# Attention layer: the last gate pieces moved into late steps by column parts, and each woven step cut into three half pieces

## The chip, the cores and the metric

The kernel runs on one core of a Trainium2 chip. The metric is the device time of one execution in microseconds, the median of several runs. The core has five engines with queues of their own: TensorE (PE, its weight loads are PEld), VectorE (DVE), ScalarE (ACT), GpSimd (POOL) and SyncE (SP, which issues DMAs). They meet only at semaphores.

## What is computed

Four layers, each `x <- x + RMSNorm(mixer(RMSNorm(x)))`, for 1024 tokens of a prompt and 8 single tokens of a second group: 1032 columns, in three parts of 344. The mixers are a gated MLP, attention, a recurrence and again a gated MLP. The change touches the attention layer alone:

```python
def project_b(h, w_in):
    z = h @ w_in                    # q (1024), k (128), v (128), gate (1024)
    ...
def mixer_b_prompt(h, w_in, sinks, w_out):
    q, k = rope(q, pos), rope(k, pos)
    scores = jnp.einsum('bnqkgd,bnskd->bnkgqs', qb, kk) * (HEAD_DIM ** -0.5)   # blocks of 128, window 128
    p = sink_softmax(scores, mask[None, :, None, None], sinks.reshape(N_KV_HEADS, Q_PER_KV))
    o = jnp.einsum('bnkgqs,bnskd->bnqkgd', p.astype(vv.dtype), vv)
    out = (o * jax.nn.silu(g)) @ w_out
```

Everything is fp32. A product is made of three matmuls of split operands: high weights by high activations, high weights by low activations, low weights by high activations.

## The kernel before

**Weights.** They come in units of 128 output features x 1024 inputs (512 KB). A ring of three slots holds them: SyncE loads `w_raw`, ScalarE writes the high half (`w_high`), VectorE the low half (`w_low`). SyncE loads unit u as soon as the result of unit u - 3 is counted (`results_at_end`).

**Units of the attention layer.** Units 0 and 1 are k and v, 2 to 5 are q and gate tiles 0 and 1, 6 to 17 in turn two q tiles and two gate tiles (6, 7 are q; 8, 9 gate; 10, 11 q; 12, 13 gate; 14, 15 q; 16, 17 gate), 18 to 25 the output product. Units 6 to 17 are not run whole but as 36 *pieces*, three per unit, one for each part of 344 columns. Piece p has 24 matmuls (8 input tiles x 3) and one of two PSUM banks; it needs piece p - 2 to be read by VectorE (`read_piece`, L1695, whose work is L1702).

**The woven loop.** 32 steps, i = 0 to 31: four groups of heads (two tiles of q) by eight blocks of 128 tokens. In step i TensorE (L862) issues a piece if the step has one, then `values(i - 1)` (L808), then the step's second piece, then `scores(i + 2)` (L777), then `turns(i)` (L795), the transposes of the probabilities. `piece_range` (L371) gives steps one and two pieces in turn, 1.5 in the mean, until piece 35 in step 22. Steps 24, 26 and 31 and the end of the loop have parts of the first two units of the output product (`out_part`, L824), steps 23 to 28 the attention of the 8 single tokens (`sample_...`).

Each step goes round the engines. VectorE: `maxima(i + 1)` (L1708, adds the mask and takes maxima, signals B; the scores two steps on need it, for their PSUM banks), the read of a first piece, `outputs(i - 1)` (L1731, times the gate), `lows(i - 2)`, the read of a second piece, `sums(i + 1)` (L1724); then for a unit that ended in the step before, `w_low` of two units on and, for a q unit, `rotate_q` (three products over 1032 columns, L1654 to L1657). ScalarE: `copies(i - 1)` (L1244, transposed probabilities out of PSUM, what values wait for), `exps(i + 1)` (L1235), `highs(i - 1)` (L1251), and for a unit that ends in this step `unit_end` (L1213): for q four DMAs that swap halves of q for the rotation (L1198), for an odd gate tile both tiles' silu (L1211, its table is another than the exponentials'), and always `w_high` of two units on. GpSimd scales the exponentials by the sums (L503), which turns need. SyncE loads the single tokens' keys behind unit 18's weights, once all q are rotated.

Each engine works its list in order, so what waits holds all behind it.

## Time and profile before

| | before |
|---|---|
| median of 3 runs | 2394.38 us (2393.76 to 2395.12) |
| the profiled execution's own time | 2395.22 us |
| its span | 2393.4 us |
| TensorE busy | 2324.8 us, 97% |
| VectorE busy | 1227.2 us, 51% |
| ScalarE busy | 891.0 us, 37% |
| GpSimd busy | 91.8 us, 4% |
| woven loop of the attention layer | 883.0 to 1152.4 us |

A row of the timeline is: start us, duration us, engine, line, operation, output<-input, shape, count, and in brackets the idle time before it with what ended it. The duration of a matmul reaches beyond the start of the next; what it costs is read from start to start. PEclk is the granted clock as a share of 2.4 GHz.

### The profile page before, as it was taken

What the parts mean: (1) busy time and instruction counts of PE and PEld (TensorE: products, weight loads), DVE (VectorE), ACT (ScalarE), POOL (GpSimd) and SP (SyncE); (2) the same over time, 40 slices, a digit from 0 to 9 for tenths busy, and PEclk for the clock granted to TensorE, in tenths of its full rate; (3) what the DMA queues carried; (4) which work ended last, traced back from release to release, by engine and by line L of the source; (5) the groups of instructions that cost most, each with busy time, mean ns of one, the idle gap of its engine ahead of it and who ended that gap; (6) DMA issues with size and microseconds to landing.
All of it is one profiled execution on the core that took longest, in us unless ns stands there. A gap on an engine that the chain in (4) does not pass through costs nothing.

```text
span 2393.4 us, 35999 instructions
## 1 busy us (share of the span) xinstructions
PE 2324.8 (97%) x15487; PEld 2238.3 (94%) x15487; DVE 1227.2 (51%) x1753; ACT 891.0 (37%) x1278; POOL 91.8 (4%) x44
## 2 busy tenths in 40 slices
PE   8999999999999899997999999999999999999997
PEld 7999999999999798886888999989999999999996
DVE  4444444454433756665256887364444544545235
ACT  6223332333332535455353366353223332333221
POOL 0000000000000002222000010000000000000000
PEclk9999999999999999997999999999999999999998
DMA  4111111111121331120222111322111111111213
GB/s 137 45 45 45 45 45 42 38 45 45 39 96 45 125 113 54 45 72 10 107 83 70 45 45 45 118 74 87 45 54 36 45 45 37 44 45 45 89 46 107
DMA packets 58494, 145.86 MB, mean 61 GB/s; under 512 B 8904, under 2 KB 29528, under 8 KB 58328
## 3 DMA queue, kind: packets, MB, share of 16 engines
q1 hardware_dynamic: 53056, 135.34, 17.2%
q10 hardware_dynamic: 5280, 8.22, 1.3%
q8 instruction: 122, 2.00, 0.3%
q14 instruction: 36, 0.29, 0.0%
HBM read 121.47 MB, written 18.37 MB: 58 GB/s over the span
## 4 chain that ended last, share of the span: by engine, by line
PE 82%; DVE 9%; ACT 4%; DVEq 3%; ACTq 1%; issue 1%; DMA 1%; SPq 0%
PE ps L528 61%; PE ps L552 7%; PE ps L773 4%; PE ps L686 2%; PE ps L610 2%; DVE x L1430 1%; DVE l_acc L1427 1%; PE ps L818 1%; DVE w_lo L1388 1%; PE ps L790 1%; PE ps L829 1%; PE ps L679 1%; ACT l_h_hi L1013 1%; DVE l_hs L1925 1%; DVEq L1429 1%
## 5 line engine op out<-in xcount | busy, mean ns | idle before, releaser
L528 PE MATMUL ps<-l_h_hi,w_hi 128*128 128x344 f32 x2448 | 526.5, 323 | 2.6 <-DVE w_lo L1388 2.6
L528 PE MATMUL ps<-l_h_lo,w_hi 128*128 128x344 f32 x2448 | 519.7, 320 | 0.0
L528 PE MATMUL ps<-l_h_hi,w_lo 128*128 128x344 f32 x2448 | 516.2, 319 | 0.0
L528 PEld LDWEIGHTS ps<-l_h_hi,w_hi 128*128 128x128 f32 x2448 | 408.9, 188 | 6.8 <-DVE w_lo L1388 3.5
L528 PEld LDWEIGHTS ps<-l_h_lo,w_hi 128*128 128x128 f32 x2448 | 414.0, 189 | 0.0
L528 PEld LDWEIGHTS ps<-l_h_hi,w_lo 128*128 128x128 f32 x2448 | 407.8, 188 | 0.0
L1388 DVE TENSOR_TENSOR w_lo<-w_raw,w_hi 128x1024 fp32r<-128x1024 f32 x182 | 226.1, 1243 | 249.8 <-ACT w_hi L962 240.5
L962 ACT ACTIVATE w_hi<-w_raw 128x1024 fp32r<-128x1024 f32 x182 | 190.8, 1049 | 117.6 <-DMA w_raw<-in_wu 79.4
L1505 DVE TENSOR_TENSOR l_tmp<-ps,rx 128x1032 f32<-128x1032 f32 x64 | 78.9, 1232 | 285.5 <-PE ps L528 285.4
L528 PE MATMUL ps<-l_y_lo,w_hi 128*128 128x344 f32 x816 | 173.2, 320 | 0.0
L528 PE MATMUL ps<-l_y_hi,w_hi 128*128 128x344 f32 x726 | 154.7, 321 | 0.8 <-DVEq L1939 0.8
L528 PE MATMUL ps<-l_y_hi,w_lo 128*128 128x344 f32 x726 | 153.1, 319 | 0.0
L1107 ACT ACTIVATE l_tmp<-l_tmp 128x1032 f32<-128x1032 f32 x32 | 34.2, 1067 | 303.9 <-DVEq L1546 303.9
L528 PEld LDWEIGHTS ps<-l_y_lo,w_hi 128*128 128x128 f32 x816 | 137.9, 189 | 0.0
L528 PEld LDWEIGHTS ps<-l_y_hi,w_hi 128*128 128x128 f32 x726 | 121.6, 188 | 1.7 <-DVEq L1939 1.1
L528 PEld LDWEIGHTS ps<-l_y_hi,w_lo 128*128 128x128 f32 x726 | 120.9, 188 | 0.0
L1112 ACT ACTIVATE l_tmp<-l_tmp 128x1032 f32<-128x1032 f32 x32 | 34.2, 1068 | 226.6 <-DVEq L1551 226.6
L1091 ACT ACTIVATE l_v<-l_v 128x1032 f32<-128x1032 f32 x32 | 34.1, 1067 | 214.9 <-DVEq L1527 214.9
L503 POOL TENSOR_TENSOR l_sc<-l_sc,l_rq 128x1024 f32<-128x1024 f32 x32 | 71.3, 2227 | 1075.1 <-DVE l_rq L1729 1075.1
L1505 DVE TENSOR_TENSOR l_v<-ps,rx 128x1032 f32<-128x1032 f32 x28 | 34.5, 1233 | 120.2 <-PE ps L528 118.1
L773 PE MATMUL ps<-l_h_hi,w_hi 128*128 128x344 f32 x288 | 95.8, 333 | 0.0
L552 PE MATMUL ps<-l_y_lo,w_hi 128*128 128x344 f32 x288 | 92.6, 322 | 0.0
(245 smaller groups left out, 3597.2 us busy)
## 6 DMA issues: line engine op xcount, KB each, us to landing
w_raw<-in_wu SPq DMA_DIRECT2D x182, 512.0 KB, 3.5
x_save<-x SPq DMA_DIRECT2D x9, 1376.0 KB, 6.1
x<-x_save SPq DMA_DIRECT2D x21, 516.0 KB, 6.9
l_sw<-l_q ACTq DMA_DIRECT2D x32, 129.0 KB, 2.8
out_y<-x SPq DMA_DIRECT2D x6, 688.0 KB, 3.6
x<-in_xt SPq DMA_DIRECT2D x4, 688.0 KB, 10.6
x<-in_xt SPq DMA_DIRECT2D x5, 516.0 KB, 6.3
x<-in_xt ACTq DMA_DIRECT2D x3, 516.0 KB, 3.7
```

What stands on the lines that cost most here:

```text
L503: nc.gpsimd.tensor_tensor(L.sc[:, i % 2], L.sc[:, i % 2], L.rq[:, i % 2].rearrange("p (h o) -> p h o", o=1).to_broadcast([P, 4, 2 * WIN]), ...
L528: mm = nc.tensor.matmul(ps[:, 3 * slot + ch, 0:CW], wt[:, w, k, :], mv[:, k, ch * CW:(ch + 1) * CW], start=(k == 0 and t == 0), stop=(k == ...
L552: mm = nc.tensor.matmul(ps[:, 3 * slot + ch, 0:CW], wt[:, u % W_RING, k, :], mv[:, k, part(ch)], start=(k == 0 and t == 0), stop=(k == KT ...
L610: mm = nc.tensor.matmul(ps[:, 3 * j + c, 0:CW], wt[:, (u + j) % W_RING, k, :], mv[:, k, part(c)], start=(k == 0 and t == 0), stop=(k == KT ...
L686: mm = nc.tensor.matmul(ps[:, 6 + b // 4, (b % 4) * P:(b % 4 + 1) * P], vt[:, b, :], L.ws[:, g, :], start=True, stop=True)
L773: mm = nc.tensor.matmul(ps[:, p % 2, 0:CW], wt[:, w % W_RING, k, :], mv[:, k, part(ch)], start=(k == 0 and t == 0), stop=(k == KT - 1 and ...
L962: nc.scalar.activation(w_hi[:, u % W_RING], w_raw[:, u % W_RING], ACT.Copy).then_inc(w_hi_done, 1)
L1091: nc.scalar.activation(tile_of(L.v, m), tile_of(L.v, m), ACT.Gelu_apprx_tanh)
L1107: nc.scalar.activation(L.tmp[:, 0, :], L.tmp[:, 0, :], ACT.Gelu_apprx_tanh).then_inc(L.u_act.sem, 1)
L1112: nc.scalar.activation(L.tmp[:, 1, :], L.tmp[:, 1, :], ACT.Silu).then_inc(L.g_act.sem, 1)
L1388: V.tensor_tensor(w_lo[:, u % W_RING], w_raw[:, u % W_RING], w_hi[:, u % W_RING], ALU.subtract).then_inc(w_lo_done, 1)
L1505: V.tensor_tensor(chunks(out), psum_result(slot), chunks(rx[:]), ALU.mult)
```

## The change

The 36 pieces get another plan (`STEP_PIECES`, `step_pieces`): entries are (piece, first input tile, end), so a piece can be halves of 12 matmuls. Steps 3 to 17 have three halves each: ahead of values, ahead of scores, ahead of turns. Steps 18 to 26 have one to three halves' worth, in the first two places. Pieces 30 to 35 (gate units 16 and 17) alternate between the two units, column part by column part, and run to step 26. VectorE reads a piece in the place in which it ends; in the third place the read stands behind the sums and ahead of `w_low` and `rotate_q`.

For pieces 30 to 35 silu is made by parts: VectorE's read writes half of the gate (g/2), ScalarE takes tanh of it into `L.th`, VectorE makes (tanh + 1) x g/2. The silu of tiles 6 and 7 goes. `w_high` and `w_low` of units 18 and 19 get places of their own (steps 22 and 22, 29 and 30). The output parts of 18 matmuls of steps 24 and 26 become four of 9 in steps 27 to 30; the single tokens' stages come two steps later.

```diff
@@ -73,7 +73,7 @@
     "ssq_mm": (CH,) * 3, "root": (CH,) * 3,
-    "x_back": (16 * (KT - A_EARLY), 16 * KT, 16 * KT), "in_done": (3 * MA, 2 * KT + 2, KT), "act_done": (MA, KT, 0),
+    "x_back": (16 * (KT - A_EARLY), 16 * KT, 16 * KT), "in_done": (3 * MA, 2 * KT + 2, KT), "act_done": (MA, KT - 2, 0), "gate_th": (0, 2 * CH, 0), "gate_done": (0, 2 * CH, 0),
     "y_hi_done": (0, 0, KT), "y_lo_done": (0, 1, KT), "h_free": (KT, 0, 0), "y_high": (MA, 0, 0), "y_low": (MA, 0, 0), "acc_done": (LAST + 3 * CH, 0, 0), "ysq_done": (LAST + 3 * CH,) * 3,
@@ -242,6 +242,8 @@
                 L.pts = at(n + "pts", o, [P, 2, P]); o += 1024
+                L.th = [at(n + "th0", o, [P, CW]), at(n + "th1", rope_at + 2 * TILE + 2080, [P, CW])]
+                o += CW * 4
                 assert o <= X_AT + KT * TILE
@@ -257,6 +259,7 @@
                 L.piece_read = s("piece_read")
+                L.gate_th, L.gate_done = s("gate_th"), s("gate_done")
             if kind == "c":
@@ -340,7 +343,8 @@
                 n = L.result_of(u) if L.kind == "c" else L.r0 + u - L.u0
-                results_at_end.append(3 * n + (5 if u in (L.u0, L.u1 - 3, L.u1 - 2) else 3))
+                by_parts = u in (L.u0, L.u1 - 3, L.u1 - 2) or (L.kind == "b" and u == L.u0 + 16)
+                results_at_end.append(3 * n + (5 if by_parts else 3))
@@ -368,13 +372,34 @@
-        def piece_range(i):
-
-            return range(min(36, 1 + (3 * i + 1) // 2), min(36, 1 + (3 * i + 4) // 2))
+        LATE = 30
+        HALF = KT // 2
+        STEP_PIECES = {0: ((2, 0, KT),), 1: ((3, 0, HALF),), 2: ((3, HALF, KT), (4, 0, KT)),
+                       18: ((27, HALF, KT), (28, 0, HALF)), 19: ((28, HALF, KT), (29, 0, KT)), 20: ((30, 0, HALF),), 21: ((30, HALF, KT), (31, 0, KT)),
+                       22: ((32, 0, HALF),), 23: ((32, HALF, KT),), 24: ((33, 0, KT), (34, 0, HALF)), 25: ((34, HALF, KT),), 26: ((35, 0, KT),)}
+        def step_pieces(i):
+            if i in STEP_PIECES or i > 18:
+                return STEP_PIECES.get(i, ())
+            halves = range(10 + 3 * (i - 3), 10 + 3 * (i - 2))
+            return tuple((h // 2, h % 2 * HALF, h % 2 * HALF + HALF) for h in halves)
+        def pieces_ended(entries):
+            return [p for p, _, end in entries if end == KT]
+        def late_end(i):
+            return [p for p in pieces_ended(step_pieces(i)) if p >= LATE]
         def piece_unit(p):
-            return 6 + p // 3
+            return 6 + p // 3 if p < LATE else 16 + p % 2
+        def piece_part(p):
+            return p % 3 if p < LATE else (p - LATE) // 2
@@ -383,7 +408,7 @@
-            return [piece_unit(p) for p in piece_range(i) if p % 3 == 2]
+            return [piece_unit(p) for p in pieces_ended(step_pieces(i)) if p < LATE and p % 3 == 2]
@@ -760,19 +785,21 @@
-                def piece(p):
-                    w, ch = u + piece_unit(p), p % 3
-                    if ch == 0:
+                def piece(p, first=0, end=KT):
+                    w, ch = u + piece_unit(p), piece_part(p)
+                    if ch == 0 and first == 0:
                         pe.wait_ge(w_lo_done, w + 1)
-                    if p >= 2:
-                        pe.wait_ge(*L.piece_read.at(p - 1))
-                    else:
-                        pe.wait_ge(evac[0], 3 * ((r + 6) // 2))
-                    for k in range(KT):
+                    if first == 0:
+                        if p >= 2:
+                            pe.wait_ge(*L.piece_read.at(p - 1))
+                        else:
+                            pe.wait_ge(evac[0], 3 * ((r + 6) // 2))
+                    for k in range(first, end):
                         for t, (wt, mv) in enumerate(((w_hi, L.h_hi), (w_hi, L.h_lo), (w_lo, L.h_hi))):
                             mm = nc.tensor.matmul(ps[:, p % 2, 0:CW], wt[:, w % W_RING, k, :], mv[:, k, part(ch)],
                                                   start=(k == 0 and t == 0), stop=(k == KT - 1 and t == 2))
-                    mm.then_inc(result, 1)
+                    if end == KT:
+                        mm.then_inc(result, 1)
@@ -860,32 +887,38 @@
                 for i in range(STEPS):
-                    now = [p for p in piece_range(i) if p >= 2]
-                    for p in now[:1]:
-                        piece(p)
-                    if i == 24:
+                    now = step_pieces(i)
+                    for p, first, end in now[:1]:
+                        piece(p, first, end)
+                    if i == 27:
                         pe.wait_ge(w_lo_done, u + 19)
                         pe.wait_ge(*L.piece_read.at(36))
                         pe.wait_ge(*L.Lo.at(19))
-                        out_part(0, 0, range(0, 6))
+                        out_part(0, 0, range(0, 3))
+                    if i == 28:
+                        out_part(0, 0, range(3, 6))
+                    if i == 29:
+                        pe.wait_ge(*L.Lo.at(22))
+                        out_part(0, 1, range(0, 3))
+                    if i == 30:
+                        out_part(0, 1, range(3, 6))
                     if i:
                         values(i - 1)
-                    for p in now[1:]:
-                        piece(p)
-                    if i == 23:
+                    for p, first, end in now[1:2]:
+                        piece(p, first, end)
+                    if i == 25:
                         sample_scores()
-                    if i == 25:
+                    if i == 27:
                         sample_turns()
-                    if i == 26:
-                        pe.wait_ge(*L.Lo.at(22))
-                        out_part(0, 1, range(0, 6))
-                    if i == 27:
+                    if i == 29:
                         sample_values()
...
                         scores(i + 2)
+                    for p, first, end in now[2:]:
+                        piece(p, first, end)
                     turns(i)
@@ -1232,6 +1265,15 @@
                     w_high(L.u0 + 6 + m)
+                def gate_tanh(p):
+                    act.wait_ge(*L.piece_read.at(p + 1))
+                    if p == LATE + 1:
+                        act.wait_ge(*L.rotated.at(KT))
+                    if p >= LATE + 2:
+                        act.wait_ge(*L.gate_done.at(p - LATE - 1))
+                    nc.scalar.activation(L.th[p % 2][:], L.gate[:, 6 + p % 2, part(piece_part(p))], ACT.Tanh).then_inc(L.gate_th.sem, 1)
                 def exps(i):
@@ -1265,7 +1307,13 @@
                         unit_end(j)
-                    if i == 24:
+                    if i == 22:
+                        w_high(L.u0 + 18)
+                    for p in late_end(i):
+                        gate_tanh(p)
+                    if i == 29:
+                        w_high(L.u0 + 19)
+                    if i == 26:
                         act.wait_ge(*L.ssE.at(1))
@@ -1693,17 +1741,28 @@
                 def read_piece(p):
-                    j, ch = piece_unit(p), p % 3
+                    j, ch = piece_unit(p), piece_part(p)
                     is_q, m = piece_tile(p)
                     dve.wait_ge(result, 3 * (r + 6) + p + 1)
-                    if not is_q and m >= 6 and ch == 0:
-
-                        dve.wait_ge(*L.kout.at(16 * 6))
-                    V.tensor_tensor((L.q if is_q else L.gate)[:, m, part(ch)], ps[:, p % 2, 0:CW], rx[:, part(ch)], ALU.mult
-                                    ).then_inc(L.piece_read.sem, 1)
+                    if p >= LATE:
+                        if ch == 0:
+                            dve.wait_ge(*L.kout.at(16 * 6))
+                        V.scalar_tensor_tensor(L.gate[:, m, part(ch)], ps[:, p % 2, 0:CW], 0.5, rx[:, part(ch)], ALU.mult, ALU.mult
+                                               ).then_inc(L.piece_read.sem, 1)
+                    else:
+                        V.tensor_tensor((L.q if is_q else L.gate)[:, m, part(ch)], ps[:, p % 2, 0:CW], rx[:, part(ch)], ALU.mult
+                                        ).then_inc(L.piece_read.sem, 1)
                     if ch == 2:
                         V.drain().then_inc(L.in_done.sem, 1)
                         V.drain().then_inc(evac[j % 2], 3)
+                def gate_silu(p):
+                    dve.wait_ge(*L.gate_th.at(p - LATE + 1))
+                    g = L.gate[:, 6 + p % 2, part(piece_part(p))]
+                    V.scalar_tensor_tensor(g, L.th[p % 2][:], 1.0, g, ALU.add, ALU.mult).then_inc(L.gate_done.sem, 1)
+                    V.drain()
@@ -1731,7 +1790,7 @@
                     dve.wait_ge(*L.PV.at(i + 1))
-                    if n == 0:
+                    if n == 0 and qd < 3:
                         dve.wait_ge(*L.act_done.at(2 * qd + 2))
@@ -1813,31 +1872,39 @@
                         maxima(i + 1)
-                    now = list(piece_range(i))
-                    for p in now[:1]:
+                    now = step_pieces(i) if i else ((1, 0, KT),) + step_pieces(0)
+                    for p in pieces_ended(now[:1]):
                         read_piece(p)
...
                         lows(i - 2)
-                    for p in now[1:]:
+                    for p in pieces_ended(now[1:2]):
                         read_piece(p)
                     if i + 1 < STEPS:
                         sums(i + 1)
+                    for p in pieces_ended(now[2:]):
+                        read_piece(p)
+                    for p in late_end(i - 1) if i else ():
+                        gate_silu(p)
+                    if i == 22:
+                        w_low(L.u0 + 18)
+                    if i == 30:
+                        w_low(L.u0 + 19)
                     for j in units_ended(i - 1) if i else []:
...
                             rotate_q(m)
-                    if i == 21:
+                    if i == 23:
                         sample_keys()
-                    if i == 23:
+                    if i == 25:
                         sample_maxima()
-                    if i == 24:
+                    if i == 26:
                         sample_normals()
-                    if i == 26:
+                    if i == 28:
                         sample_probs()
-                    if i == 28:
+                    if i == 30:
                         sample_outputs()
```

## Rows read from the trace of the kernel before

**Rows 1.** Busy time by stretch: steps 0-17, 18-22, 23-31; columns in the first line.
```profile
core 0: us, PE busy (x) PEld busy (x) DVE busy (x) ACT busy (x) POOL busy (x), PEclk, DMA share, GB/s
883.00:1043.20 160.20, 158.84 (x1259) 139.28 (x1257) 101.34 (x312) 86.02 (x225) 41.55 (x19) 1.00 0.18 51
1043.20:1088.70 45.50, 44.73 (x353) 39.21 (x352) 34.87 (x94) 21.80 (x59) 12.05 (x6) 1.00 0.22 61
1088.70:1152.40 63.70, 46.97 (x369) 33.77 (x367) 32.05 (x132) 35.04 (x98) 17.66 (x9) 0.73 0.02 8
```

**Rows 2.** Timeline of TensorE over a step with two pieces.
```profile
974.06 0.43 PE L773 MATMUL ps<-l_h_hi,w_hi 128*128 128x344 f32 x1
974.33 0.32 PE L773 MATMUL ps<-l_h_lo,w_hi 128*128 128x344 f32 x1
974.49 0.32 PE L773 MATMUL ps<-l_h_hi,w_lo 128*128 128x344 f32 x1
...
978.04 1.08 PE L818 MATMUL ps<-l_pt,l_vtok 128*64 128x256 f32 x8
979.06 0.42 PE L773 MATMUL ps<-l_h_hi,w_hi 128*128 128x344 f32 x1
...
983.04 1.13 PE L790 MATMUL ps<-l_kd,l_q 64*128 64x256 f32 x8
984.00 0.66 PE L804 MATMUL ps<-ident,l_sc 64*128 64x64 f32 x16
984.59 0.42 PE L773 MATMUL ps<-l_h_hi,w_hi 128*128 128x344 f32 x1
```

**Rows 3.** Timeline of TensorE: values in steps without pieces ahead of them.
```profile
1091.85 1.97 PE L818 MATMUL ps<-l_pt,l_vtok 128*64 128x256 f32 x8 [3.14 <-ACT l_pt L1248]
...
1130.39 1.97 PE L818 MATMUL ps<-l_pt,l_vtok 128*64 128x256 f32 x8 [1.11 <-ACT l_pt L1248]
...
1136.35 1.08 PE L818 MATMUL ps<-l_pt,l_vtok 128*64 128x256 f32 x8 [1.11 <-ACT l_pt L1248]
```

**Rows 4.** Timeline of VectorE: the sums of two steps that follow each other.
```profile
1139.69 0.16 DVE L1727 TENSOR_TENSOR l_rq<-l_mx 128x4 f32<-128x4 f32 x1 [1.42 <-ACTq L1242]
...
1144.45 0.16 DVE L1727 TENSOR_TENSOR l_rq<-l_mx 128x4 f32<-128x4 f32 x1 [1.41 <-ACTq L1242]
```

**Rows 5.** Timeline of VectorE: sums, low weights, rotation, the next maxima.
```profile
973.30 0.15 DVE L1727 TENSOR_TENSOR l_rq<-l_mx 128x4 f32<-128x4 f32 x1
...
973.62 1.20 DVE L1388 TENSOR_TENSOR w_lo<-w_raw,w_hi 128x1024 fp32r<-128x1024 f32 x1
974.73 2.93 DVE L1654 TENSOR_TENSOR l_sw<-l_sw,l_sin 128x1032 f32<-128x1032 f32 x1
...
978.88 1.23 DVE L1657 TENSOR_TENSOR l_q<-l_q,l_sw 128x1032 f32<-128x1032 f32 x1
980.39 0.48 DVE L1716 CUSTOM_DVE_ANT_0 l_sc<-ps,l_mask,l_sink 128x256 f32<-128x256 f32 x1 [0.28 <-issue]
```

**Rows 6.** Timeline of ScalarE behind it, and TensorE's values that wait.
```profile
982.47 0.51 ACT L1239 ACTIVATE l_sc<-l_sc,l_mx 128x256 f32<-128x256 f32 x1 [7.27 <-DVEq L1722]
...
984.82 2.46 ACTq L1198 DMA_DIRECT2D l_sw<-l_q  x4
...
988.29 1.00 ACT L1248 ACTIVATE l_pt<-ps 128x1024 f32<-128x1024 f32 x1
...
989.35 1.08 PE L818 MATMUL ps<-l_pt,l_vtok 128*64 128x256 f32 x8 [0.71 <-ACT l_pt L1248]
```

**Rows 7.** Timeline of steps 0 to 2: first piece of step 1, a copy, exponentials.
```profile
898.52 0.42 PE L773 MATMUL ps<-l_h_hi,w_hi 128*128 128x344 f32 x1
...
901.12 1.01 ACT L1248 ACTIVATE l_pt<-ps 128x1024 f32<-128x1024 f32 x1
...
913.42 0.51 ACT L1239 ACTIVATE l_sc<-l_sc,l_mx 128x256 f32<-128x256 f32 x1 [7.22 <-DVEq L1722]
```

**Rows 8.** Timeline of ScalarE in step 22: the last silu and the load ahead.
```profile
1086.63 1.28 ACT L1211 ACT_TABLE_LOAD   x1
1087.93 2.02 ACT L1211 ACTIVATE l_gate<-l_gate 128x1032 f32<-128x1032 f32 x2
```

## What I expect, and how it is worked out

> **What bounds the kernel now.** I first read the stretches: the attention layer's woven loop runs from 883.0 to 1152.4 us, 269.4 us in 32 steps. TensorE is busy for 158.84 of 160.20 us in steps 0 to 17 and for 44.73 of 45.50 us in steps 18 to 22, but only for 46.97 of 63.70 us in steps 23 to 31, and the granted clock there is 0.73 on average, so the two levels (2.4 and 1.2 GHz) take turns [rows 1]. All the rest of the span lies outside the change, so the question is only how long the 269.4 us become.
>
> Next I read one step on TensorE. A piece of 24 products takes 3.98 us from its start to that of what follows, the first product 0.27 and the others 0.16 (0.157 over many); values take 1.02, scores 0.96 ahead of turns, turns 0.59 [rows 2]. Scores with a piece behind them take 1.06: a piece starts 0.06 ahead of the end shown for values (1.08, and 1.02 to the next start), and scores show 1.13. So the work of the loop at the full clock is: 36 pieces x 3.98 = 143.3; 32 values x 1.02 = 32.6; 32 scores, 30.9; 32 turns x 0.59 = 18.9; the four parts of the output product (48 products x 0.157 and 0.21 of edges for each part) 8.4; the three sample groups about 3.6, an estimate. Sum 237.7. Of the 31.7 us that are left, 1.4 + 0.8 are idle before step 23 and 16.7 after [rows 1]. The remaining 12.8 us is what the lower clock adds: values take 1.97 us in it and not 1.08 [rows 3].
>
> What makes the idle time? Up to step 22 hardly anything: the pieces hide it. Without pieces a step is a ring of VectorE and ScalarE: maxima, then the exponentials, then the sums, and VectorE starts the next maxima only behind the sums. That ring is 4.76 us from sums to sums [rows 4]. A step of values, scores and turns alone is 2.6 us of TensorE. With half a piece it is 4.7, about what the ring needs. This is what speaks for the change.
>
> **The change, part by part.**
>
> (1) *Splitting costs edges.* A half piece is 3.98 - 12 x 0.157 = 2.1 us, so a split adds 0.18 to 0.2 us. A step of three halves instead of one and a half pieces adds 1.5 x 0.18 and the 0.10 of scores that now have a piece behind them, 0.37 us [rows 2]; 15 steps (3 to 17) give 5.6. Pieces 3, 28, 30, 32 and 34 and the two output parts of 18 products are split too: 7 x 0.18 = 1.3. Together **+6.9 us**, all on TensorE and so on the path. From below the edge could be nothing where no wait stands at the cut; but every cut here has values, scores or turns in it, so I take the row.
>
> (2) *VectorE is held by the third half.* In even steps from 4 to 16 the third half ends a piece, and its read stands ahead of the low weights and the rotation of q. Before, those followed the sums: from sums to the next maxima 7.1 us with w_lo (1.20), the sin product (2.93) and two more of 1.2 [rows 5]. Only the first runs slow, and GpSimd works beside it there; behind the third half it no longer does, so I take 1.23 for it, and w_lo plus rotation is 5.0 us (6.7 if it stays slow). Walk such a step with its start at 0: TensorE runs 2.08, values to 3.1, half to 5.2, scores to 6.2, third half to 8.3, turns to 8.9. VectorE reads the third half until 8.95, rotates until 13.95, and its maxima are good 2.1 us later (980.39 to 982.47), at 16.05 [rows 5, 6]. The scores of the next step want them at 8.9 + 5.2 = 14.1. That is a wait of **2.0 us** in each of steps 5, 11 and 13 (rotations of units 7, 10, 11), from 0 to 3.7. Before, the same scores came behind two whole pieces, and the rotation was hidden. In steps 6, 8, 14 and 16 only w_lo (1.20) follows, and nothing is late.
>
> (3) *ScalarE has less cover.* The q swap issues four DMAs, 2.46 us of its queue, then a high weight, and only then the copy that values wait for; with four microseconds of piece ahead of values TensorE still waited 0.71 us [rows 6]. Ahead of values there are now only 2.1 us. In steps with q's end in second place the half behind the scores makes up for it, except behind the late scores of step 11: 1.1 us in step 12. Step 1: the copy ends at 902.13 and the half that begins at 898.52 ends at 900.6: 1.5 us. Step 2: maxima are good at 913.4 [rows 7], and 3b, values and piece 4 end at 911.8: 1.6 us; before, a further piece stood there. Together steps 1 to 13: 3 x 2.0 + 1.1 + 3.1 = **10.2 us**, against 1.4 that go.
>
> (4) *Steps 18 to 22.* Piece 29 is whole and ends unit 15 in step 19; swap, weight and copy follow as at 984.82 to 989.29, and the copy is ready 6.9 us behind the end of the piece (before 6.3, now the maxima of step 20 are some 0.6 later). Scores, turns and half a piece cover 3.6: values wait **3.3 us**. The rotation then makes scores(23) late by 1.7, and the two tanh ahead of the copy make values(21) late by 0.9.
>
> (5) *The last gates.* Two silu of 1.0 us, a table load of 1.28 and the load of 1.28 for the exponentials go; they stood ahead of the 3.14 us wait [rows 3, 8]. Six tanh of 344 columns come (0.5 each by the exponential's 0.51 for 256 columns and the copy's 1.00 for 1024, from 0.4 to 0.6 [rows 6]) and six VectorE products of about 0.55, in the ring: 3.3 us of VectorE spread over steps 22 to 27. [...]
>
> (6) *Steps 23 to 31, walked the same way.* Ring 4.76 plus what stands in it: sample_keys 3.0, maxima of the samples 2.7, normals 2.7, the gate products 0.6 each, w_lo 1.2. Waits of TensorE: step 23 1.4, 26 0.2, 27 3.7 (copy behind tanh, exponentials of the samples and high rows; then the normals, then maxima), 28 1.0, 29 0.4, 30 0.5, 31 2.1 (copy behind w_high(19), moved ahead of it). Sum 9.3, in place of 16.7 [rows 1]. The weight DMAs of units 18 to 20 are issued over ten microseconds ahead of need; SyncE's new wait for unit 16 (piece 34, step 25) holds only unit 19's load, wanted in step 30 by VectorE.
>
> **The sum.** 237.7 + 6.9 + 10.2 + (3.3 + 1.7 + 0.9) + 9.3 = 270.0 us, against 269.4: +0.6 at the full clock throughout. The lower clock still costs something: the 3.14 us wait before was followed by values at 1.97 us, and so will the new one of 3.3 be; the sparse steps 27 to 31 follow. A step at the lower clock took 5.96 us and not 4.76 [rows 3, 4], 1.2 more; two such stretches of one to two steps cost about 3. So **+3.6 us**. The profiled execution took 2395.22 us, 0.84 over the median of the three; on the median 2394.38 this gives **2398.0 us**. What the tail gains, edges and early waits eat.
>
> [...]
>
> **Rivals.**
> (A) The forecast: gains and costs even out, -4.8 to +4.8 us. 0.42.
> (B) Slower, by the clock: the waits of steps 19 to 23 and 27 to 31 let it fall as often as before, and now half pieces and output halves are in those stretches and double. It decides once three stretches occur: 0.6 + 3 x 2.5 = +8, at most 0.6 + 12.8 = +13.4, so about 2403 and up to 2408. For it: 0.73 in the same steps before. Against: 9.3 us idle and not 16.7. 0.31.
> (C) Slower, since the change's point fails: tanh is not in the loaded set, and five switches there and back put at least 5 x 1.28 = 6.4 us into the ring: 2404. 0.07.
> (D) Faster: VectorE isn't late. If rotation and maxima fit under the cover (for instance because the reads of third halves come earlier against the sums than I walked), 7.1 us of steps 5, 11, 12, 13 go, and the clock stays up: 0.6 - 7.1 = -6.5: 2387.9. For it: the rotation itself gets shorter by 1.7. Against: the order on VectorE is fixed. 0.20.
>
> **Numbers.** About 0.2% (4.8 us) can be told from no change. Faster 0.20 (D), same 0.42 (A), slower 0.38 (B, C). The range reaches from the middle of D, 2387, to 2406, inside B: it takes in rotations at 0 to 3.7 us each (-6 to +5) and one to three clock stretches.
>
> **What would show it.** Edges: first product of a half 0.27 behind its start, halves 2.1 us. (2): TensorE's scores waiting on VectorE's maxima, about 2 us, in steps 5, 11, 13, and w_lo right behind a read of a third half; the sin product at 1.2 us. (3), (4): values waiting for the copy in steps 1, 12 and 20. (5): no table load between tanh and exponentials, two loads fewer on ScalarE. (6): idle in the last nine steps near 9 us and more of it at 1.00 granted clock. I am wrong if scores don't wait in the early steps (then faster), or if the granted clock in the tail stays under 0.8 (then slower).

## The result and the profile after

The kernel after the change takes 2403.32 us, the median of 6 runs (2399.56 to 2404.93), and the kernel before, beside it on the same chip, 2394.40 (6 runs, 2393.76 to 2395.26): 8.9 us or 0.37% slower, ratio 1.0035 with a 95% interval of 1.0026 to 1.0045. It lies inside my range, but 5.3 us over the predicted time, and over the 0.2% that I had drawn as the border of "same". The profiled execution took 2403.29 us, its span 2401.3. One run of all that follow, in the experiment "weights moved", took 2816.04 us at a granted clock of 0.75 and is left out of its figures.

The same view as [rows 1], of the kernel after, with the stretches cut where steps 17 and 22 now end (columns: length, busy time and instructions by engine, granted clock, share and rate of the DMA):

```profile
core 0: us, PE busy (x) PEld busy (x) DVE busy (x) ACT busy (x) POOL busy (x), PEclk, DMA share, GB/s
883.00:1060.20 177.20, 169.79 (x1246) 140.54 (x1244) 96.11 (x310) 86.03 (x225) 36.87 (x19) 0.96 0.16 44
1060.20:1100.30 40.10, 35.00 (x284) 28.63 (x280) 29.70 (x81) 19.48 (x58) 9.35 (x4) 0.96 0.23 61
1100.30:1162.00 61.70, 52.40 (x455) 41.29 (x452) 41.93 (x152) 35.04 (x101) 18.84 (x9) 0.94 0.06 18
```

The loop takes 279.0 us and not 269.4. Against [rows 1] the last nine steps are 2.0 us shorter and steps 18 to 22 are 5.4 shorter, as the change wants it, and the tail runs at a granted clock of 0.94 and not 0.73. Steps 0 to 17, where before nothing was wrong, are 17.0 us longer. Half a piece (2.0 us of work) has passed from there to the next stretch, so the early steps really lost 19.0.

What the early steps wait for now. TensorE's waits there, from its timeline (start, duration, operation, and in brackets the idle time and who ended it):

```profile
902.49 1.08 PE L845 MATMUL ps<-l_pt,l_vtok 128*64 128x256 f32 x8 [1.93 <-ACT l_pt L1290]
...
940.35 1.36 PE L817 MATMUL ps<-l_kd,l_q 64*128 64x256 f32 x8 [1.83 <-DVEq L1781]
...
997.63 1.13 PE L817 MATMUL ps<-l_kd,l_q 64*128 64x256 f32 x8 [1.82 <-DVEq L1781]
...
1018.96 1.47 PE L817 MATMUL ps<-l_kd,l_q 64*128 64x256 f32 x8 [1.83 <-DVEq L1781]
```

These are values of step 1 and the scores of steps 5, 11 and 13. What holds VectorE ahead of step 5's is in its own timeline:

```profile
932.72 0.52 DVE L1754 TENSOR_TENSOR l_gate<-ps,rx 128x344 f32<-128x344 f32 x1 [3.50 <-PE ps L799]
933.16 1.21 DVE L1436 TENSOR_TENSOR w_lo<-w_raw,w_hi 128x1024 fp32r<-128x1024 f32 x1
934.29 1.23 DVE L1702 TENSOR_TENSOR l_sw<-l_sw,l_sin 128x1032 f32<-128x1032 f32 x1
...
938.24 0.48 DVE L1775 CUSTOM_DVE_ANT_0 l_sc<-ps,l_mask,l_sink 128x256 f32<-128x256 f32 x1 [0.28 <-issue]
```

VectorE idles 3.50 us for the third half, reads it, and only then turns to the low weights and the rotation. The sin product takes 1.23 us here and not the 2.93 of [rows 5]. Still the maxima begin only at 938.24, and the scores that need them at 940.35, when TensorE has had nothing to do for 1.83 us.

And what TensorE does behind such a wait, its timeline after the one of step 5:

```profile
941.64 0.65 PE L799 MATMUL ps<-l_h_hi,w_hi 128*128 128x344 f32 x1
942.09 0.49 PE L799 MATMUL ps<-l_h_lo,w_hi 128*128 128x344 f32 x1
942.38 0.49 PE L799 MATMUL ps<-l_h_hi,w_lo 128*128 128x344 f32 x1
```

The half piece runs from 941.64 to 945.02, where the turns begin, 3.4 us for 12 products and not 2.1; its products are 0.285 us apart and not 0.157. The stretches of the loop in which this happens, seven of 3.4 us each, at 903.6, 941.1, 999.1, 1019.6, 1081.1, 1135.7 and 1156.1; four of them (same columns as above):

```profile
903.60:907.00 3.40, 3.40 (x26) 2.86 (x27) 2.81 (x5) 1.87 (x7) 1.97 (x1) 0.50 0.00 0
941.10:944.50 3.40, 3.40 (x14) 2.86 (x11) 0.80 (x4) 2.76 (x9) 1.45 (x1) 0.50 0.05 20
...
1081.10:1084.50 3.40, 3.03 (x14) 1.72 (x16) 0.94 (x5) 2.79 (x11) 0.00 (x0) 0.50 0.00 0
...
1156.10:1159.50 3.40, 3.40 (x26) 2.47 (x22) 1.35 (x4) 0.42 (x1) 1.18 (x1) 0.51 0.00 0
```

The granted clock of 0.50 is the level that the prediction and two expectations call 1.2 GHz, and 1.00 is their 2.4 GHz; no view gives a frequency. The products of 344 columns are 0.285 us apart there, 1.21 columns in each ns, and 0.157 us apart at a granted clock of 1.00, 2.19 columns. Four of the seven lie in the early steps, each right behind one of the four waits above, and before there was none (1.00 in [rows 1]). Before, 34.0 us in four stretches were low, all of them from 1091.1 on; now it is 23.8 us. So the change made the low time shorter, and moved half of it to where TensorE is never free. A stretch full of products loses 3.4 x (1 - 0.157 / 0.285) = 1.5 us.

With that the 17.0 us of the early steps add up: waits of 7.4 in place of 1.4 (+6.0), four low stretches (+6.1), and edges. The edges are read from a step without waits, the turns of two steps in TensorE's timeline of after:

```profile
945.02 0.71 PE L831 MATMUL ps<-ident,l_sc 64*128 64x64 f32 x16
945.66 0.42 PE L799 MATMUL ps<-l_h_hi,w_hi 128*128 128x344 f32 x1
...
954.00 0.71 PE L831 MATMUL ps<-ident,l_sc 64*128 64x64 f32 x16
954.64 0.42 PE L799 MATMUL ps<-l_h_hi,w_hi 128*128 128x344 f32 x1
```

The step takes 954.64 - 945.66 = 8.98 us. A step with one and a half pieces took 8.54 before: 10.53 with two by [rows 2], less 1.99, half of a piece. That is 0.44 a step, 6.6 in 15 steps. 6.0 + 6.1 + 6.6 - 2.0 = 16.7 of the 17.0.

The middle and the tail are kept short of what they could be by a few large waits: of values in step 20, of scores in steps 23 and 27 and of values in step 31. ScalarE ahead of the first, and TensorE's values behind it:

```profile
1076.62 2.79 ACTq L1231 DMA_DIRECT2D l_sw<-l_q  x4
1079.45 1.06 ACT L995 ACTIVATE w_hi<-w_raw 128x1024 fp32r<-128x1024 f32 x1 [2.50 <-issue]
1080.41 1.00 ACT L1290 ACTIVATE l_pt<-ps 128x1024 f32<-128x1024 f32 x1
```
```profile
1081.47 1.97 PE L845 MATMUL ps<-l_pt,l_vtok 128*64 128x256 f32 x8 [3.47 <-ACT l_pt L1290]
...
1106.59 1.13 PE L817 MATMUL ps<-l_kd,l_q 64*128 64x256 f32 x8 [2.81 <-DVEq L1781]
...
1135.65 2.08 PE L817 MATMUL ps<-l_kd,l_q 64*128 64x256 f32 x8 [1.67 <-DVEq L1781]
...
1155.43 0.88 PE L845 MATMUL ps<-l_pt,l_vtok 128*64 128x256 f32 x6 [2.61 <-ACT l_pt L1290]
```

### The profile page after: what moved, and what is told of

It reads as the page before. It is cut to its first block, busy times and chain, and to the rows that moved or that the text cites. A ratio compares the mean times of both kernels' runs of the same rounds, so it can differ in the third digit from the quotient of the medians.

```text
span 2401.3 us, 36017 instructions
## 1 busy us (share of the span) xinstructions
PE 2331.0 (97%) x15487; PEld 2236.9 (93%) x15487; DVE 1226.6 (51%) x1759; ACT 888.8 (37%) x1280; POOL 85.6 (4%) x44
## 4 chain that ended last, share of the span: by engine, by line
PE 81%; DVE 10%; ACT 3%; DVEq 3%; ACTq 1%; issue 1%; DMA 1%; SPq 0%
PE ps L553 61%; PE ps L577 7%; PE ps L799 4%; PE ps L711 2%; PE ps L635 2%; DVE x L1478 1%; DVE l_acc L1475 1%; PE ps L817 1%; PE ps L856 1%; DVE w_lo L1436 1%; DVE l_sc L1775 1%; PE ps L845 1%; PE ps L704 1%; ACT l_h_hi L1046 1%; DVE l_hs L1992 1%
## 5 line engine op out<-in xcount | busy, mean ns | idle before, releaser
L553 PE MATMUL ps<-l_h_hi,w_lo 128*128 128x344 f32 x2448 | 516.2, 319 | 0.0
L553 PE MATMUL ps<-l_y_lo,w_hi 128*128 128x344 f32 x816 | 173.2, 320 | 0.0
L528 POOL TENSOR_TENSOR l_sc<-l_sc,l_rq 128x1024 f32<-128x1024 f32 x32 | 65.1, 2033 | 1091.8 <-DVE l_rq L1788 1091.8
L799 PE MATMUL ps<-l_h_hi,w_lo 128*128 128x344 f32 x288 | 93.6, 325 | 0.0
## 6 DMA issues: line engine op xcount, KB each, us to landing
x<-in_xt SPq DMA_DIRECT2D x4, 688.0 KB, 10.2
```

The costliest lines, as they stand in the source:

```text
L528: nc.gpsimd.tensor_tensor(L.sc[:, i % 2], L.sc[:, i % 2], L.rq[:, i % 2].rearrange("p (h o) -> p h o", o=1).to_broadcast([P, 4, 2 * WIN]), ...
L553: mm = nc.tensor.matmul(ps[:, 3 * slot + ch, 0:CW], wt[:, w, k, :], mv[:, k, ch * CW:(ch + 1) * CW], start=(k == 0 and t == 0), stop=(k == ...
L799: mm = nc.tensor.matmul(ps[:, p % 2, 0:CW], wt[:, w % W_RING, k, :], mv[:, k, part(ch)], start=(k == 0 and t == 0), stop=(k == KT - 1 and ...
```

## The experiments

My theory after the result: the loss is made in steps 1 to 17 by three things of about equal size, edges, VectorE's order, and the low clock that follows its waits. The rivals are that the halves cost what they cost wherever VectorE reads them (edges alone), and that the gate parts of the tail (tanh, products) eat the gain there. Each kernel is compared with the kernel before, run beside it (its medians were 2394.66, 2394.75 and 2394.89 in the three sets); edits are against the kernel after unless I say otherwise.

**Only VectorE's order turned.** The read of the third half goes behind low weights and rotation, in all steps:

```diff
-                    for p in pieces_ended(now[2:]):
-                        read_piece(p)
                     for p in late_end(i - 1) if i else ():
...
                             rotate_q(m)
+                    for p in pieces_ended(now[2:]):
+                        read_piece(p)
```

> The changed kernel with one order turned round on VectorE: the low weights and the rotation stand ahead of the read of the piece that ends in third place, not behind it. My theory is that the changed kernel's three waits of 1.83 us of scores on maxima (steps 5, 11, 13), and the stretches at 1.2 GHz behind them (some 1.6 us each), come from that order: about 10 us go, 2393 us. The rival, that the cuts themselves and their places cost the time, expects 2401 to 2403. A second rival, that the third read is then late and holds TensorE's next piece, expects waits of piece products on VectorE and 2398 or more.

Measured: 2394.59 us (10 runs, 2392.95 to 2396.49), ratio 0.9999 (0.9989 to 1.0008). The order alone makes the 8.7 us. Its stretches, cut as before:

```profile
883.00:1049.90 166.90, 163.02 (x1242) 135.00 (x1240) 100.66 (x310) 85.94 (x225) 43.11 (x19) 1.00 0.16 47
1049.90:1090.00 40.10, 35.61 (x278) 29.15 (x278) 29.70 (x81) 19.28 (x58) 9.36 (x4) 0.91 0.24 61
1090.00:1153.10 63.10, 54.32 (x461) 43.06 (x457) 42.16 (x152) 35.44 (x103) 18.84 (x9) 0.92 0.06 18
```

The early steps are 10.3 us shorter than with the change as it is, and at 1.00 throughout (what lies behind step 17 is 1.4 us longer, with 17.1 us of low stretches and not 10.2): the scores of steps 5, 11 and 13 wait no more, 10.1 us by 5.5 of waits and three low stretches of 1.5. The low stretch of step 1 is absent here as well, where TensorE waits 1.57 us and not 1.93, but the wait of step 2 (1.54) that it had swallowed is back, so this evens out. The sin product is slow again, as VectorE's timeline shows, and it costs nothing, because it runs under the third half:

```profile
929.29 2.92 DVE L1702 TENSOR_TENSOR l_sw<-l_sw,l_sin 128x1032 f32<-128x1032 f32 x1
...
934.83 0.52 DVE L1754 TENSOR_TENSOR l_gate<-ps,rx 128x344 f32<-128x344 f32 x1 [0.17 <-issue]
935.27 0.47 DVE L1775 CUSTOM_DVE_ANT_0 l_sc<-ps,l_mask,l_sink 128x256 f32<-128x256 f32 x1
```

The maxima begin at 935.27 and not at 938.24.

**Only one rotation turned, that of step 4.** It prices one wait with what follows it:

```diff
-                    for p in pieces_ended(now[2:]):
+                    for p in pieces_ended(now[2:]) if i != 4 else ():
                         read_piece(p)
...
                             rotate_q(m)
+                    for p in pieces_ended(now[2:]) if i == 4 else ():
+                        read_piece(p)
```

> The changed kernel with the order on VectorE turned round in step 4 alone, so that only the first of the three waits of 1.83 us (scores of step 5) goes. One third of the 8.7 us that all three gave: 2400 to 2401 us, with a wait and a low-clock stretch left in each of steps 11 and 13 and none in step 5. If the clock stretches came from something else than these waits, the one in step 5 would stay and only 1.8 us would go.

Measured: 2401.00 us (9 runs, 2399.65 to 2402.32), ratio 1.0026 (1.0016 to 1.0035), 2.3 less than after. TensorE's scores of steps 5, 11 and 13, in its timeline:

```profile
938.70 1.14 PE L817 MATMUL ps<-l_kd,l_q 64*128 64x256 f32 x8
...
994.47 1.14 PE L817 MATMUL ps<-l_kd,l_q 64*128 64x256 f32 x8 [1.83 <-DVEq L1781]
...
1015.83 1.69 PE L817 MATMUL ps<-l_kd,l_q 64*128 64x256 f32 x8 [1.81 <-DVEq L1781]
```

The wait and the low stretch of step 5 are gone, those of the other two stay, only some 3.1 us earlier than in the kernel of the change (994.47 and not 997.63): 1.8 of wait and the rest clock. Behind step 17 part of it is lost again: the low stretches there last 17.1 us and not 10.2, and values of step 31 start only 1.3 us earlier (1154.10 and not 1155.43). So one rotation is worth 2.3 us by the medians and 3.1 at its place in the trace, and three of them make up most or all of the 8.7.

**Whole pieces in the early steps, the tail as after.** The plan of pieces is changed back for steps 0 to 17; pieces 28 and 29 are whole in steps 18 and 19:

```diff
-        STEP_PIECES = {0: ((2, 0, KT),), 1: ((3, 0, HALF),), 2: ((3, HALF, KT), (4, 0, KT)),
-                       18: ((27, HALF, KT), (28, 0, HALF)), 19: ((28, HALF, KT), (29, 0, KT)), 20: ((30, 0, HALF),), 21: ((30, HALF, KT), (31, 0, KT)),
+        STEP_PIECES = {0: ((2, 0, KT),), 18: ((28, 0, KT),), 19: ((29, 0, KT),), 20: ((30, 0, HALF),), 21: ((30, HALF, KT), (31, 0, KT)),
...
-            halves = range(10 + 3 * (i - 3), 10 + 3 * (i - 2))
-            return tuple((h // 2, h % 2 * HALF, h % 2 * HALF + HALF) for h in halves)
+            return tuple((p, 0, KT) for p in range(1 + (3 * i + 1) // 2, 1 + (3 * i + 4) // 2))
```

> The changed kernel, but steps 0 to 17 have the whole pieces of the kernel before, 1.5 a step, pieces 28 and 29 stand whole in steps 18 and 19, and from step 20 all is as changed. My theory (the early halves lose 17 us up to the turns of step 17, the new tail wins 7.6 behind them) expects 2386 to 2389 us, 3.2 us of edges less. The rival that the tail is what lost (the 3.5 us wait behind piece 29, the parts, the tanh) expects 2394 us or more.

Measured: 2387.35 us (7 runs, 2387.09 to 2390.47), ratio 0.9970 (0.9959 to 0.9982): faster than before by 7.3 us, and 7.2 less than with the halves and VectorE's order turned. What is between those two is the edges (6.6 by the step above) and the waits of steps 1 and 2. Its stretches:

```profile
883.00:1042.60 159.60, 157.98 (x1253) 138.41 (x1251) 100.70 (x312) 86.03 (x225) 41.49 (x19) 1.00 0.18 51
1042.60:1083.40 40.80, 34.32 (x272) 28.68 (x268) 29.01 (x80) 19.02 (x57) 10.98 (x5) 0.92 0.19 53
1083.40:1144.40 61.00, 52.31 (x455) 41.51 (x451) 42.04 (x152) 35.15 (x101) 18.85 (x9) 0.94 0.06 18
```

The half of the change that lies behind step 17 is the whole gain, and it needs nothing of the other half. Since the tanh and the products are in this kernel too, they can't be what makes the changed kernel slower than before.

**The other half alone.** The kernel before, with three half pieces in steps 1 to 17; pieces 27b to 35 in steps 18 to 22 and the tail as before:

```diff
+        HALF = KT // 2
+        STEP_PIECES = {0: ((2, 0, KT),), 1: ((3, 0, HALF),), 2: ((3, HALF, KT), (4, 0, KT)), 18: ((27, HALF, KT), (28, 0, KT)),
+                       19: ((29, 0, KT), (30, 0, KT)), 20: ((31, 0, KT),), 21: ((32, 0, KT), (33, 0, KT)), 22: ((34, 0, KT), (35, 0, KT))}
...
                         scores(i + 2)
+                    for p, first, end in now[2:]:
+                        piece(p, first, end)
                     turns(i)
...
                         sums(i + 1)
+                    for p in pieces_ended(now[2:]):
+                        read_piece(p)
```

> The kernel before with the three halves in steps 1 to 17 and nothing of the tail's change: pieces 27 to 35 whole in steps 18 to 22, silu, output parts and sample stages as before. My theory expects the whole early loss and no gain: 2394.4 plus 15 to 17, so 2409 to 2412 us. The rival that the tail lost expects the halves to cost their edges alone: about 2400 us.

Measured: 2411.60 us (4 runs, 2408.86 to 2411.88), ratio 1.0065 (1.0050 to 1.0080): 16.9 slower than before. Its early stretch is as long as that of after (the same three waits of scores with a low stretch behind each, and 1.51 and 1.54 us of wait in steps 1 and 2 without one), its tail is like that of before, at a low clock:

```profile
883.00:1060.10 177.10, 168.57 (x1248) 139.59 (x1246) 96.14 (x310) 86.03 (x225) 36.87 (x19) 0.97 0.16 44
...
1107.40:1169.20 61.80, 44.49 (x369) 31.53 (x367) 32.69 (x133) 35.33 (x98) 18.56 (x9) 0.78 0.02 8
```

The two halves of the change add up: 16.9 - 7.3 = 9.6 us, against 8.9 measured.

**Three halves in two places.** The third half moves up behind the second, ahead of the scores, and all reads of pieces ahead of the sums:

```diff
-                    for p, first, end in now[1:2]:
+                    for p, first, end in now[1:]:
                         piece(p, first, end)
...
-                    for p, first, end in now[2:]:
-                        piece(p, first, end)
                     turns(i)
...
-                    for p in pieces_ended(now[1:2]):
+                    for p in pieces_ended(now[1:]):
                         read_piece(p)
...
-                    for p in pieces_ended(now[2:]):
-                        read_piece(p)
```

> The changed kernel with the third half of each step moved up behind the second, ahead of scores, so that nothing stands ahead of turns and all reads stand ahead of the sums. My theory expects that the rotations hide again (the waits of steps 5, 11, 13 go, with their low clock) and that part of the edges goes too (about 3 us): 2388 to 2391 us. If cutting pieces costs by itself more than the 0.2 us that I take, 2396 or more.

Measured: 2400.59 us (9 runs, 2396.88 to 2402.23), ratio 1.0025 (1.0015 to 1.0035): only 2.7 less than after, and 10 to 13 more than I expected. TensorE's timeline, its waits and the turns of a step without any:

```profile
940.49 1.13 PE L817 MATMUL ps<-l_kd,l_q 64*128 64x256 f32 x8 [1.02 <-DVEq L1779]
...
969.94 0.66 PE L831 MATMUL ps<-ident,l_sc 64*128 64x64 f32 x16
...
978.58 0.66 PE L831 MATMUL ps<-ident,l_sc 64*128 64x64 f32 x16
...
1002.79 1.08 PE L845 MATMUL ps<-l_pt,l_vtok 128*64 128x256 f32 x8 [3.13 <-ACT l_pt L1288]
```

Two things are to be seen. The scores still wait, 1.0 us in place of 1.8: the rotation starts sooner, but runs beside GpSimd again, and its sin product takes 2.93. And values wait now (in steps 6, 8, 12 and 14, 0.87 to 3.13 us), because ahead of turns no half is left that gave ScalarE time for swap, weight and copy. So I had seen the third half as a burden alone, while it also covers ScalarE. Of the edges my theory is borne out: the step takes 8.64 us from turns to turns, 0.1 over the 8.54 of before and 0.34 under 8.98. Between two halves that follow each other the products go on at 0.16 us; the 0.1 goes with two places of pieces in each step where before there were 1.5 in the mean. What costs is that TensorE changes from pieces to another stage and back.

**The middle improved.** The kernel of "whole pieces", with another plan behind step 17 (28 and 29 both in step 18, 30 in 19, and in steps 20 to 26 other places for the cuts):

```diff
-        STEP_PIECES = {0: ((2, 0, KT),), 18: ((28, 0, KT),), 19: ((29, 0, KT),), 20: ((30, 0, HALF),), 21: ((30, HALF, KT), (31, 0, KT)),
-                       22: ((32, 0, HALF),), 23: ((32, HALF, KT),), 24: ((33, 0, KT), (34, 0, HALF)), 25: ((34, HALF, KT),), 26: ((35, 0, KT),)}
+        STEP_PIECES = {0: ((2, 0, KT),), 19: ((30, 0, KT),), 20: ((31, 0, KT), (32, 0, HALF)), 21: ((32, HALF, KT),),
+                       22: ((33, 0, HALF),), 23: ((33, HALF, KT),), 24: ((34, 0, KT),), 25: ((35, 0, HALF),), 26: ((35, HALF, KT),)}
```

> The kernel with whole pieces in the early steps (e2_whole_early, 2387.4 us) and a plan that covers the rotations later too: pieces 28 and 29 both in step 18, as before the change, 30 whole in step 19, 31 and half of 32 in step 20, then halves of 32 and 33, 34 whole in step 24, halves of 35. My theory: what stands ahead of scores and values decides, so the waits of 3.42 us (scores, step 18) and 2.36 us (values, step 20) go but for some 1 us, and a stretch at 1.2 GHz with them: 2380 to 2383 us. If a wait moves elsewhere for each that goes, 2386 or more.

Measured: 2385.25 us (5 runs, 2383.18 to 2388.42), ratio 0.9960 (0.9945 to 0.9974), 9.5 under before: the lowest median of all. In steps 18 to 22 two waits (3.42 and 2.36 us, on scores and values) are replaced by small ones of 0.2 to 1.0, and the stretch runs at 1.00:

```profile
1042.70:1081.60 38.90, 35.52 (x295) 29.99 (x293) 30.25 (x83) 18.82 (x56) 11.30 (x5) 1.00 0.21 55
1081.60:1142.90 61.30, 50.78 (x428) 40.05 (x427) 40.07 (x149) 35.14 (x103) 18.67 (x9) 0.89 0.06 18
```

Over the kernel it started from it gains 2.1 us and not the 4 to 7 that I had expected: the tail gives 0.3 back and its clock goes to 0.89. The two intervals overlap, so by the times alone that it is the faster of the two is not shown; the trace shows only where its waits went.

**Weights moved in the tail.** That kernel, with the weights of unit 18 made in step 24 and not 22, those of unit 19 in 28 and 29:

```diff
-                    if i == 22:
+                    if i == 24:
                         w_high(L.u0 + 18)
...
-                    if i == 29:
+                    if i == 28:
                         w_high(L.u0 + 19)
...
-                    if i == 22:
+                    if i == 24:
                         w_low(L.u0 + 18)
-                    if i == 30:
+                    if i == 29:
                         w_low(L.u0 + 19)
```

> The same with the high and low weights of unit 18 in step 24 (under a whole piece) instead of 22, and of unit 19 in steps 28 and 29 instead of 29 and 30. Theory: in the sparse steps each microsecond on VectorE or ScalarE is in the ring, and so the waits of 2.8 us (scores, step 23) and 2.6 us (values, step 31) shrink by about a microsecond each: 2 to 4 us less than e5_pair_at_18. The rival that weights there are hidden gives the same time.

Measured: 2386.80 us (7 runs, 2383.97 to 2389.60), ratio 0.9966 (0.9955 to 0.9976), no gain; the intervals overlap. TensorE's waits only change places; the largest two are now 2.96 us (scores at 1110.75) and 1.98 (values at 1140.32). My reading is that what stands in the ring stands there, in whichever step.

**Without the gate parts.** The kernel of "whole pieces" without the tanh and the products that follow (the gates of pieces 30 to 35 stay linear; that part of the computation is left out):

```diff
-                    for p in late_end(i):
-                        gate_tanh(p)
...
-                    for p in late_end(i - 1) if i else ():
-                        gate_silu(p)
```

> e2_whole_early without the tanh on ScalarE and the gate product on VectorE for the last six pieces: their gate stays linear, which leaves out part of the computation. It prices the new gate parts. If they are in the ring, as I forecast (3.3 us of VectorE, 2.7 of ScalarE), 2383 to 2385 us; if they are hidden, 2387.

Measured: 2385.37 us (5 runs, 2384.95 to 2388.79), ratio 0.9965 (0.9952 to 0.9978), 2.0 less. The intervals overlap, so 2 us is an estimate that is not clear of noise, but the parts surely don't cost the whole 8.9: with the kernel of "whole pieces", which has them and is faster than before, the second rival falls.

**The copy of step 20 first.** ScalarE makes the high weights of unit 17 behind the copy and not ahead of it:

```diff
-                    w_high(L.u0 + j + 2)
+                    if j != 15:
+                        w_high(L.u0 + j + 2)
...
                         copies(i - 1)
+                    if i == 20:
+                        w_high(L.u0 + 17)
```

> The changed kernel with one edit: ScalarE's high weights of unit 17 stand behind the copy of step 19, not ahead of it. My theory is that values' wait of 3.47 us in step 20 is ScalarE's list, swap and weights ahead of the copy: it shrinks by the 1.05 us of the weights, and the next exponentials start as late as before, so that little of it stays: 2402 to 2403 us. If the wait were bound by the piece or by VectorE it would stay 3.47 us. A low-clock stretch behind it that goes too would give 2400 to 2401.

Measured: 2402.17 us (6 runs, 2400.73 to 2405.02), ratio 1.0031 (1.0019 to 1.0043). The wait of values falls from 3.47 to 2.64 us; the time by 1.1, inside the scatter. ScalarE's timeline there:

```profile
1075.89 0.62 ACTq L1231 DMA_DIRECT2D l_sw<-l_q  x1
1076.61 1.02 ACT L1291 ACTIVATE l_pt<-ps 128x1024 f32<-128x1024 f32 x1 [2.61 <-issue]
```

By these rows the larger part of that wait is the swap: four DMA issues of 0.6 us each, one of which is shown, for which the engine stands 2.61 us, with the copy right behind. No run takes the swap away.

## Why the prediction was right or wrong

**(1) Edges.** Forecast 0.37 us a step and 6.9 in all; measured 0.44 a step, 6.6 for 15 steps, and 7.9 with the other splits at their forecast price. Right, 1.0 short. The bound from below, "nothing where no wait stands at the cut", was shown to hold for halves that follow each other directly (0.16 us from product to product).

**(2) VectorE held by the third half.** Right in place, order and size: scores wait in steps 5, 11 and 13, 1.83, 1.82 and 1.83 us against 2.0; w_lo right behind the read, the sin product 1.23. The runs that turn the order, in one step and in all, show it to be the cause.

**(3) Copies early.** Step 1: 1.93 against 1.5. The wait of step 2 (1.6) did not come: at the low clock behind the wait of step 1 TensorE itself was late enough; where the clock stayed up, with VectorE's order turned, it is there with 1.54. Step 12's (1.1) did not come either, and step 11 ran slow ahead of it; with VectorE's order turned, and no low stretch there, values of step 12 do wait 0.77. Early waits 7.4 against 10.2.

**(4) Steps 18 to 22.** Values of step 20 wait 3.47 (3.3 forecast) behind swap and weight as walked; scores of step 21 wait 0.76 where I had 1.7, values of step 22 wait 0.68 where I had 0.9, and 0.19 comes in step 19. 5.1 against 5.9.

**(5) The gates.** The trace of after has no table load at the tanh (L1275); two that follow each other take 0.86 us, in ScalarE's timeline of after:

```profile
1095.93 0.86 ACT L1275 ACTIVATE l_th<-l_gate 128x344 f32<-128x344 f32 x2
```

The loads of ScalarE by line, for silu and for the exponentials (line, count, busy time and mean ns of one, idle time ahead); both lines had four before:

```profile
L1244 ACT ACT_TABLE_LOAD x3 | 3.8, 1283 | 8.6 <-issue 8.6
L1281 ACT ACT_TABLE_LOAD x3 | 3.8, 1283 | 0.1
```

Rival (C) falls: the six tanh add no load, and the exponentials have one less. Of what a switch costs the rows show the load, 1283 ns, with the silu 0.02 us behind it in [rows 8]. The parts cost some 2 us by their own run, which is not clear of noise.

**(6) The last nine steps.** Waits 9.2 us against 9.3, as a sum nearly exact; one by one they were off both ways, and that the sum fits is luck: step 23 has 3.0 and not 1.4 (2.81 of it scores), step 31 2.6 and not 2.1, but step 27 3.1 and not 3.7, and steps 28 to 30, where I had 1.9 together, have none.

**The lower clock: the step that failed.** My sum had two low stretches worth 3 us, one behind the wait of step 20 and one in the sparse steps, and full clock throughout the early steps. Put together with what the trace shows: work 237.7, edges 7.9, waits 21.7, seven low stretches. TensorE is busy for 23.4 of their 23.8 us, at 0.45 lost of each microsecond, 10.5. That is 277.8 of 279.0; 1.2 stays unexplained. Against my 273.0 (237.7 + 6.9 + 25.4 + 3.0): edges +1.0, waits -3.7, clock +7.5, rest +1.2, together +6.0. The time outside the loop was 1.5 us shorter than in the profiled execution before, so 4.5 are left over against my 2398.8 for it. The clock term alone is larger than the miss: that the waits came out 3.7 shorter than I had them hides part of it, and that is luck. I had priced the early waits at 2.0 us as if TensorE went on at the full clock behind them, although [rows 3] show values at 1.97 us, and not 1.08, behind a wait of only 1.11 us. A wait of 1.83 us in steps where TensorE bounds costs about 1.8, and 1.5 more when a low stretch follows, as it did behind ten of eleven such waits; by the run with one rotation turned it is 2.3 to 3.1 together.

**The rivals.** The size was that of (B), 2403, whose chance I had put under that of (A). Its mechanism, the clock, was the right one, but half its place was wrong: three low stretches lie in steps 19 to 31, as it said, and cost 4.4 us, but in the tail the clock rose from 0.73 to 0.94; the other four, 6.1 us, fell where neither (A) nor (B) had looked. (D) was wrong: its condition, VectorE not late, is just what the kernel with VectorE's order turned fulfils, and it takes 2394.6, not 2387.9, since the edges and the waits of steps 1 and 2 remain.

## What to carry to other kernels

Before cutting work into parts to fill later waits, look whether the steps that the cut passes through had any idle time: here the first 18 of 32 steps had 1.4 us together, and a plan that cuts only from step 18 on turns a loss of 8.9 us into a gain of 7.3 to 9.5. A read that an in-order engine must do for a late part belongs behind the work that can go ahead of it; turning that order was worth 8.7 us. And price a new wait in a stretch full of products with the lower clock that may follow it, and not by its own length alone: here 1.5 us behind ten of the eleven early waits of 1.8 us, and nothing behind the eight of 1.51 to 1.78 us.

## What the runs showed of the hardware

- **The granted clock falls to 0.50 behind single short waits in a dense stretch, though not behind all.** In the kernel after, stretches of 3.4 us at 0.50 follow waits of 1.82, 1.83, 1.83 and 1.93 us, with TensorE busy with products or scores nearly all the time ahead of each. The four kernels that keep the waits of 1.81 to 1.83 us on scores have eleven of them, and a low stretch follows ten: the last one of "the copy of step 20 first" has none, and its scores take 1.14 us, as TensorE's timeline shows:

```profile
1017.54 1.14 PE L817 MATMUL ps<-l_kd,l_q 64*128 64x256 f32 x8 [1.82 <-DVEq L1784]
```

  Of the waits of steps 1 and 2, the two of 1.93 us have a low stretch behind them and the eight of 1.51 to 1.78 us, in four kernels, have none. With three halves in two places the wait of 3.13 us has one and those of 0.87 to 1.58 us have none. The wait of 2.81 us of step 23 was not followed by one in the kernel after (its scores took 1.13 us) and was in five other kernels. What decides is open.
- **VectorE beside GpSimd.** The sin product takes 2.92 us beside GpSimd's product in one kernel and 1.23 in the other, and GpSimd's product 2.79 and 1.89. The low weights and GpSimd's product in the timeline of the kernel with VectorE's order turned, and then GpSimd's in that of the change:

```profile
928.18 1.20 DVE L1436 TENSOR_TENSOR w_lo<-w_raw,w_hi 128x1024 fp32r<-128x1024 f32 x1
...
928.34 2.79 POOL L528 TENSOR_TENSOR l_sc<-l_sc,l_rq 128x1024 f32<-128x1024 f32 x1 [5.56 <-DVE l_rq L1788]
```
```profile
929.30 1.89 POOL L528 TENSOR_TENSOR l_sc<-l_sc,l_rq 128x1024 f32<-128x1024 f32 x1 [5.56 <-DVE l_rq L1788]
```

  The low weights, which start first, take 1.20 us as they do alone (1.21) and end at 929.38; 1.89 us from there, GpSimd's time in the change with VectorE idle beside it, is 931.27, and GpSimd ends at 931.13. The sin product, issued at 929.29, ends at 932.21, 1.08 us behind GpSimd's end, and alone takes 1.23. These times are near those of three products one after the other. That each waits for the one before is my estimate from them; no run shows what they share. In the code the sin product waits for the semaphore of the swap alone, so these two engines meet elsewhere than at semaphores too.
- **A cut costs where the stage changes.** A step of three halves spread over three places takes 0.44 us more than the mean step of one and a half whole pieces, and 0.10 us more where two of the halves stand together; between those two the products go on at 0.16 us.
